# A routed-expert transformer layer: rows spread over the DMA queues, one sum in memory instead of two, and another order of the blocks

## What is computed

```python
h = modulate(rms_norm(x, ffn_norm_g), sh2, sc2)          # 512 x 1024
scores = sigmoid(h @ w_router)                            # 512 x 64
idx = top-8 experts of each token (4 of 8 groups of experts allowed)
w   = scores[idx] / sum * 2.5
routed[t] = sum over the 8 chosen e: w[t, e] * (silu(h[t] @ wg[e]) * (h[t] @ wu[e])) @ wd[e]
shared    = (silu(h @ wgs) * (h @ wus)) @ wds
out = x + g2 * (routed + shared)
```

## Time and profile before

| | us |
|---|---|
| median of 3 executions | 1282.87 |
| lowest and highest of them | 1282.39, 1285.67 |
| the profiled execution, its own time | 1285.91 |
| its span, first to last instruction | 1284.1 |

### The profile page before, as it was taken

One profiled execution on the slowest core, in us unless ns is written; L12 is line 12 of the kernel. 1 busy time (PEld: TensorE's weight loads), 2 busy tenths in 40 slices (PEclk: granted clock), 3 DMA queues, 4 the chain that ended last, 5 costly groups with the idle time before them and its releaser, 6 DMA issues.

```text
span 1284.1 us, 14047 instructions
## 1 busy us (share of the span) xinstructions
PE 1203.1 (94%) x4705; PEld 606.4 (47%) x4705; DVE 462.0 (36%) x1239; ACT 197.6 (15%) x452; POOL 193.3 (15%) x221
## 2 busy tenths in 40 slices
PE   6999999999999999998899998889999898999985
PEld 3444544444888544444444444333444343444442
DVE  2536557100666222555233323222323232233322
ACT  4110001011665001120001100000100010011100
POOL 0000000000221000100022323222222112223212
PEclk9999999999999999998899999988999899999998
DMA  8966661112100302167789999999999999989952
GB/s 275 368 217 229 219 231 65 66 65 83 50 0 1 131 1 106 72 256 290 278 294 364 383 386 378 382 364 375 370 300 379 386 363 391 384 291 381 358 135 35
DMA packets 88910, 311.52 MB, mean 243 GB/s; under 512 B 12400, under 2 KB 38160, under 8 KB 64912
## 3 DMA queue, kind: packets, MB, share of 16 engines
q1 hardware_dynamic: 72480, 272.77, 55.0%
q0 software_dynamic: 14784, 35.68, 11.8%
q10 hardware_dynamic: 1584, 2.27, 0.5%
HBM read 295.47 MB, written 34.08 MB: 257 GB/s over the span
## 4 chain that ended last, share of the span: by engine, by line
PE 80%; DMA 14%; DVE 2%; issue 1%; SPq 1%; ACT 1%; POOL 0%; DVEq 0%; POOLq 0%; ACTq 0%
PE PS L1718 21%; PE PS L1429 19%; PE PS L1739 11%; DMA R_HSA<-w_up_e 5%; DMA R_Z<-w_up_e 5%; PE PS L1597 4%; PE PS L1568 4%; PE PS L1704 3%; PE PS L1501 3%; PE PS L1477 2%; PE PS L1412 2%; DMA out<-second_sum 2%; DMA R_G<-h_rows,gidx 2%; PE PS L1607 2%; PE PS L1489 1%
## 5 line engine op out<-in xcount | busy, mean ns | idle before, releaser
L1429 PE MATMUL PS<-R_WT,R_HSA 128*128 128x512 f32 x576 | 248.2, 592 | 0.0
L1429 PEld LDWEIGHTS PS<-R_WT,R_HSA 128*128 128x128 f32 x576 | 109.3, 190 | 135.9 <-issue 135.8
L1265 DVE TENSOR_TENSOR R_G<-R_G,PS 128x256 f32<-128x256 f32 x50 | 30.4, 608 | 356.6 <-ACT R_G L864 356.6
L1718 PE MATMUL PS<-R_Z,R_G 128*64 128x512 f32 (+1 forms) x384 | 137.5, 603 | 13.0 <-DMA R_XM<-w_up_e 9.7
L1718 PE MATMUL PS<-R_WT,R_G 128*64 128x512 f32 (+1 forms) x352 | 129.1, 636 | 18.9 <-DMA R_WT<-w_up_e 10.9
L657 POOL DMA_INDIRECT R_G<-h_rows,gidx x54 | 56.3, 1042 | 431.6 <-DVE gidx L1254 370.5
L869 ACT ACTIVATE R_G<-PS 128x256 f32<-128x256 f32 x50 | 19.2, 383 | 556.2 <-PE PS L1726 556.2
L1286 DVE SCALAR_TENSOR_TENSOR R_G<-PS,slx,R_XM 128x512 f32<-128x512 f32 x100 | 74.9, 750 | 64.5 <-PE PS L1739 64.5
L1718 PEld LDWEIGHTS PS<-R_Z,R_G 128*64 128x64 f32 (+1 forms) x384 | 52.6, 161 | 92.9 <-issue 92.9
L1718 PE MATMUL PS<-R_XM,R_G 128*128 128x512 f32 (+1 forms) x192 | 88.0, 613 | 0.0
L1718 PEld LDWEIGHTS PS<-R_WT,R_G 128*64 128x64 f32 (+1 forms) x352 | 46.2, 163 | 84.7 <-issue 84.7
(11 more groups left out here) (256 smaller groups left out, 1318.6 us busy)
## 6 DMA issues: line engine op xcount, KB each, us to landing
R_Z<-w_gate_e SPq DMA_DIRECT2D x22, 1024.0 KB, 17.2
R_Z<-w_up_e SPq DMA_DIRECT2D x22, 1024.0 KB, 27.7
R_Z<-w_down_e SPq DMA_DIRECT2D x22, 1024.0 KB, 24.9
R_WT<-w_gate_e SPq DMA_DIRECT2D x21, 1024.0 KB, 16.6
R_WT<-w_up_e SPq DMA_DIRECT2D x21, 1024.0 KB, 30.1
R_WT<-w_down_e SPq DMA_DIRECT2D x21, 1024.0 KB, 27.1
R_WT<-ada_w SPq DMA_DIRECT2D x18, 1024.0 KB, 7.5
R_WT<-w_in SPq DMA_DIRECT2D x9, 2048.0 KB, 10.3
```

Source lines behind the costliest of these rows:

```text
L1265: dve.tensor_tensor(AR[:, b, :].rearrange("p (k d) -> p d k", k=2), by_line(SIL[:, b, :], 2), by_line(PS[:, b, F:2 * F], 2), ALU.mult).the ...
L1429: ins = mm(PS[:, t, :], HT[:, k, P * t:P * t + P], WR[:, b, k, :], start=k == 0, stop=k == KD - 1)
L1718: ins = mm(PS[w * h:w * h + w, b, :].rearrange("p (g n) -> p g n", g=2), XT[:, b, k, w * h:w * h + w], WGU[n][:, k], start=k == 0, stop=k ...
```

## The change

It does seven things.

- **Slots.** A new constant `slots` (loaded to `SLOTS` by one DMA of 224 KB on SyncE's queue, ahead of w_router) gives a block's rows other slot numbers: with 128 rows, rows 0, 8, 16, ... take slots 1 to 16, rows 1, 9, 17, ... take 17 to 32, and so on, so that the filled rows lie evenly over 16 groups of neighbouring rows. In every second single (`turned`) the groups count from the other end. A pair does this in each half with groups of four rows, the second half turned. For a narrow block, `onehot` now writes 96 slots and not 128.
- **One sum.** `second_sum`, `sum_order`, `sums_before` and `join_sums` are gone. All scatters add to `out`, and each waits until the one before has landed (`added`). A pair's second half waits for its first half on GpSimd.
- **Shared expert.** Its result is added to `out` by five accumulating DMAs from GpSimd (`add_shared`), between gather(1) and gather(2), in place of ScalarE's plain writes.
- **Start of GpSimd's loop.** gather(2) and gather(3) follow the shared adds; the waits for them to land stay before the first scatter.
- **Order of blocks.** `ORDER` spells out the 50 blocks; the pairs reach to the last one. `TAIL` is gone. The start is (0,), (1,), (30, 31), (7,), (8,), (32, 33), and the end is (58, 59), (27,), (60, 61), (28,), (29,), (62, 63). Three pairs in a row stand in two places.
- **Waits of VectorE.** `take_o` waits for the one count.
- **No drain.** The block is made with `no_gpsimd_drain=True`.

```diff
-TAIL = 6
+ORDER = "PWWPWWSWPWPPPWWPWWPSWWWPWWWPWWPPPWWPSPWPWWP"
 def block_order():
-    wide = [(j,) for j in range(7, NFULL - TAIL)]
-    half = [(j, j + 1) for j in range(NFULL, E, 2)]
-    apart = {3: [(2,), (64,)], 9: [(3,), (4,), (65, 66)], 15: [(5,), (6,), (67, 68)]}
+    wide = iter((j,) for j in range(7, NFULL))
+    half = iter((j, j + 1) for j in range(NFULL, E, 2))
+    apart = iter([[(2,), (64,)], [(3,), (4,), (65, 66)], [(5,), (6,), (67, 68)]])
     order = [(0,), (1,)]
-    for n, cols in enumerate(wide):
-        order += apart.get(n, []) + [cols] + half[n:n + 1]
-    return order + [(j,) for j in range(NFULL - TAIL, NFULL)]
+    for kind in ORDER:
+        order += next(apart) if kind == "S" else [next(wide if kind == "W" else half)]
+    return order
...
+ADDED = [sum(len(cols) for cols in COLS[:n]) for n in range(NM + 1)]
...
+def spread_slots(rows, turned):
+    row = np.arange(rows)
+    engine = row // (rows // 16)
+    return row % (rows // 16) * 16 + (15 - engine if turned else engine) + 1
...
-        block = st.enter_context(nc.Block())
+        block = st.enter_context(nc.Block(no_gpsimd_drain=True))
...
+        def turned(j, b):
+            return (j - PAIRS[j]) % 2 if isinstance(j, int) and j < NM else b
...
+        def added(j):
+            if isinstance(j, int) and j <= NM:
+                return 16 * ADDED[j]
+            return 16 * (j + (ADDED[NM] - NM))
...
+            sp.dma_start(SLOTS, a["slots"]).then_inc(s_ws, 16)
...
             def scatter(i, b):
                 j = 2 * i + b
                 pool.wait_ge(s_oe, 2 * j + 2)
                 pool.wait_ge(s_ri, copies(j + 1))
-                into = INTO[j] if isinstance(j, int) and j < NM else (0,)
-                for n in into:
-                    need(pool, s_sum[n], sums(n, j) + (16 if isinstance(j, int) and j == NM - TAIL else 0))
+                need(pool, s_sum, added(j))
                 settle(pool)
-                if len(into) == 1:
-                    add_rows(into[0], ridx[b], OB[0:rows(j), b, :])
+                if len(columns(j)) == 1:
+                    add_rows(ridx[b], OB[0:rows(j), b, :])
                 else:
-                    add_rows(0, ridx[b], OB[0:P // 2, b, :])
-                    add_rows(1, rhigh[b], OB[P // 2:P, b, :])
-            def join_sums():
-                pool.wait_ge(s_sum[1], sums(1, NM))
-                pool.wait_ge(s_sum[0], sums(0, NM - TAIL))
-                pool.dma_start(a["out"], sum_dram, accum_op=ALU.add, max_dma_last_dim=4 * D).then_inc(s_sum[0], 16)
-            for j in range(4):
-                gather(j, j % 2)
+                    add_rows(ridx[b], OB[0:P // 2, b, :])
+                    pool.wait_ge(s_sum, added(j) + 16)
+                    add_rows(rhigh[b], OB[P // 2:P, b, :])
+            def add_shared(t, ready):
+                pool.wait_ge(s_sx, ready)
+                for piece, at in SHARED_PIECES[t]:
+                    pool.dma_start(a["out"][P * t:P * (t + 1), at:at + piece.shape[1]], piece, accum_op=ALU.add)\
+                        .then_inc(s_sout[t % 2], 16)
+            gather(0, 0)
+            gather(1, 1)
+            pool.wait_ge(s_out, 16 * NT)
+            add_shared(1, 2)
+            add_shared(0, 4)
+            add_shared(2, 6)
+            add_shared(3, 8)
+            gather(2, 0)
+            gather(3, 1)
...
                 gather(j + 4, j % 2)
-                if j == NM - TAIL:
-                    join_sums()
                 scatter(j // 2, j % 2)
...
-            write_shared(1, 2)
-            write_shared(0, 4)
-            write_shared(2, 6)
             take_xt(0, 0)
             take_xt(1, 1)
-            write_shared(3, 8)
...
             def take_o(i, j, b):
-                if isinstance(j, int) and 2 <= j < NM:
-                    for n in INTO[j - 2]:
-                        dve.wait_ge(s_sum[n], sums(n, j - 1))
-                elif not isinstance(j, int) or j >= 2:
-                    dve.wait_ge(s_sum[0], sums(0, j - 1))
+                if not isinstance(j, int) or j >= 2:
+                    dve.wait_ge(s_sum, added(j - 1))
```

More of the change, by code:

```diff
@@ L123 @@
 C_N = C_SEL + HA
+S_WIDE = (0, P)
+S_NARROW = (2 * P, 2 * P + NARROW)
+S_N = 2 * P + 2 * NARROW
+def spread_slots(rows, turned):
+    row = np.arange(rows)
+    engine = row // (rows // 16)
+    return row % (rows // 16) * 16 + (15 - engine if turned else engine) + 1
 def constants():
@@ L134, in constants @@
     c[:, C_ONE:C_ONE + P] = 1.0
-    c[:, C_SLOT:C_SLOT + P] = f + 1
+    slots = np.zeros((P, S_N), np.float32)
+    for turned in range(2):
+        c[:, C_SLOT + P // 2 * turned:C_SLOT + P // 2 * turned + P // 2] = spread_slots(P // 2, turned)
+        slots[:, S_WIDE[turned]:S_WIDE[turned] + P] = spread_slots(P, turned)
+        slots[:, S_NARROW[turned]:S_NARROW[turned] + NARROW] = spread_slots(NARROW, turned)
     token = p + P * np.arange(NT)[None]
@@ L157, in constants @@
     causal[:, S - P:] = np.where(f > p, NEG, 0.0)
-    return c, causal
+    return c, causal, slots
 def build(nc, a):
@@ L337, in build @@
         s_gat = [sem(f"gathered{b}") for b in range(2)]
-        s_sum = [sem(f"added_to_sum{n}") for n in range(2)]
+        s_sum = sem("rows_added")
         s_ah, s_ohd, s_sl, s_xt, s_xtd, s_xta, s_gu, s_silu, s_act, s_at, s_ate, s_dn, s_oe, s_ri = map(sem, (
@@ L345, in build @@
         s_out = sem("residual_written")
-        s_sout = [sem(f"shared_written{b}") for b in range(2)]
+        s_sout = [sem(f"shared_added_to_out{b}") for b in range(2)]
         s_etab = sem("main_experts_ready")
@@ L660, in gather, with add_rows @@
                     bounds_check=S - 1, oob_is_err=False).then_inc(s_gat[b], 16)
-            def add_rows(n, index, part):
+            def add_rows(index, part):
                 pool.indirect_dma_start(
-                    out=sum_dram if n else a["out"],
+                    out=a["out"],
                     out_offset=bass.IndirectOffsetOnAxis(ap=index[0:part.shape[0], 0:1], axis=0),
                     in_=part, in_offset=None, compute_op=ALU.add,
-                    bounds_check=S - 1, oob_is_err=False).then_inc(s_sum[n], 16)
+                    bounds_check=S - 1, oob_is_err=False).then_inc(s_sum, 16)
             def scatter(i, b):
@@ L1801 @@
         give(name, array if name == "c" else array.reshape(array.shape[1:]))
-    for name, array in zip(("consts", "causal"), constants()):
+    for name, array in zip(("consts", "causal", "slots"), constants()):
         give(name, array)
```

24 lines of the change are left out of this document (10 added, 14 removed).

## The result

The changed kernel takes **1272.97 us** in the median (1268.80 to 1281.28, 11 runs) beside 1284.83 of the kernel before (11 runs): a ratio of 0.9915, 95% interval 0.9894 to 0.9935. It is faster by 0.9%, a quarter of what was forecast (1234 us). The time lies outside the range of 1220 to 1266. The profiled execution took 1276.11 us with a span of 1274.0; that of before had a span of 1284.1.

The account below looks back on a forecast made before the run. TensorE and the DMA engines were taken to bound the stage in turn, TensorE alone after the change: 1198.4 + 3 + 4 + 17.6 + 12.0 = 1235 us of span, so 1234 us, range 1220 to 1266.

Parts of the forecast that it names:

- Spread slots: Rows on DMA engines: spreading cuts q0's cost per byte from 1.96 to 1.40 of q1's, weights' work to 564 us.
- the work of 611 us: DMA engines from 600 us on: 259.9 MB, with q0's bytes priced at 1.96, at 425 GB/s.
- The third bound, the scatters: Chain of 69 scatters one at a time: 572 us against TensorE's 590, so hidden, with 3% to spare.
- a second half alone, 6: A pair's second scatter, issued alone: lands in 6 us, between 5.4 and 7.5.
- A single, 8.2: A single block's scatter: lands in 8.2 us with spread rows, 9.7 before, plus 0.95 to the next start.
- The second rival: Scatter chain paces, since spreading shortens no landing: chain 619 us, time 1265 us, kernel still gains; chance 0.13.
- its stated sign: VectorE's waits before ridx for a landing of out, over 10 us in all, would show rival 2 or 3.
- The first rival: Spread gives nothing and DMA engines pace: last weights at 1222 us, time 1250 us; chance 0.22.
- Rival 3: Scatter chain at the old landings of 8.8 us: 673 us, time 1318 us; chance 0.07 slower, 0.03 gain cancelled.
- The need for weights is level to the end: New block order without join: same bytes, TensorE's floor puts gate_up of block 49 at 1198.4 us.
- Shared rows: Five accumulating DMAs on GpSimd before gather(2): nothing if weights leave room, 8 us if not, 3 taken.
- The end: From gate_up of block 49: 17.6 us to VectorE's last product, then 12.0, the 6.28 us drain gone.

Follow-up runs that it names:

- e4: The kernel before with the slots table and the spread one-hots, nothing else; 1281.01 us, ratio to before 0.9957.
- e2: The changed kernel with the two sums and the join of before put back; order, spread and missing drain stay; 1272.36 us, ratio to before 0.9893.
- e12: The kernel with two sums, new order, spread slots and no drain, its join left out, so the second sum never reaches the output; 1264.74 us, one execution.
- e8: The kernel before with the new block order alone; two sums, join, drain and rows in place kept; 1288.76 us, ratio to before 1.0023.
- e7: The kernel before without GpSimd's drain at the end, nothing else changed; 1279.38 us, ratio to before 0.9958.
- e6: The changed kernel with scatters as plain writes, their addition left out; 1230.53 us, one execution.
- e13: The kernel with two sums, join, new order, spread slots and no drain, its scatters as plain writes, the join's addition kept; 1240.30 us, one execution.
- e9: Against the changed kernel: two sums, an order with eight singles last, the join in four pieces ahead of the 8th, 6th, 4th and 2nd block from the end; 1276.03 us.

## Why the prediction was wrong, point by point

**The failed step: "Spread slots".** It stands in two bounds, the DMA engines' work and a single's landing in the chain of scatters. The working took the measured price of a q0 byte (1.96 of q1's) and put it down to rows that crowd on few DMA engines, so that a spread would divide it by 1.4. A price was measured, its cause was assumed. The spread left it unchanged (22.1% before and after in e4). The addition in memory was most of the cause: by the queues' shares the price is 1.59 with it and 1.10 without, and the kernel then takes 1230.5 us. That is nearly the forecast's time, by another way: it was the time of a kernel whose DMA engines have room. The 1.96 itself is high, since the shares of the earlier trace rows give 1.61, but the work of 611 us is low: by the shares of the earlier trace rows, (69.3 + 22.2)% of 684.1 us, it is 626.

The prediction never priced the addition as something that could be the cause. The Trainium skill, "DMA: Bandwidth & Descriptors", section "SDMA does more than copy", says that each DMA engine has small compute units inline with the stream, an add among them; it gives no price, and the runs give one. The rule of the Trainium skill, "DMA: Bandwidth & Descriptors", section "The descriptor swizzle", by which each engine writes fixed partitions of a 128-partition transfer, was weighed against the spread. It came out on the right side (landings of 8.5 and 8.4 us with and without the spread), but no row shows which engine a row goes to, so the runs don't confirm it as the reason.

**Where the 38.5 us lie.** Block 49 was forecast at 1198.4 + 3 + 4 = 1205.4 and started at 1243.9. It is made of: block 2 at 642.5, where 644.3 + 3 was taken, -4.8; TensorE's own pace in the new order, 547.3 / 46 = 11.90 us a step in place of 11.79, +5 (both orders have nearly the same blocks, and over its first 12 steps, none of them late, before took 11.83, so up to 2 of these 5 may belong to the eight steps behind 11.79); lateness of 41.0 and 1.3 in the last step, where 4 were allowed, +38.3.

**The third bound, the scatters.** This is the bound that paced the changed kernel. The term "a second half alone, 6" measured 7.7 (median of 14 in 660 to 1180 us, 7.2 to 8.1), just above the upper bound of 7.5. "A single, 8.2" measured 10.0 (median of 24), as in before (10.3): it too rested on the spread. Over all 69 scatters the second halves took 7.2 us in the mean, which makes 23 of the 57 us between 572 and 629; the others took 8.6 where 7.9 had been put in, 37 us; shorter gaps gave 4 back. The second rival's working gave 619, and its stated sign came true: VectorE's waits ahead of ridx in 640 to 1280 us are 166 us, far over 10. It lacked those 23 us, and its other landings were 10 us too long in all. The prediction had also said that it is wrong if mean landings stay above 7.5: the mean of all 69 was 8.2. The first rival (the spread gives nothing, weights pace, 1250 us) was right on its cause too, and e2 and e12 show its limit with 28 to 30 us of lateness. Its time was early by the 15 us that the sum of the work lacked: the last weights landed at 1232.1 us in e12 and not at 1222. Neither rival was weighed together with the other, and each alone gave too early a time. Both true together had no case and no chance in the sum; the range ended at the one rival's own time. Rival 3 (1318 us, mean landing 8.8) had the landings among weights right (mean 8.7 in 660 to 1180 us) and its time too high: towards the end, with no weights moving, they fell to 3.5 to 5.2 us, and the mean of all, 8.2, is just under the 8.3 at which it would have cancelled the gain.

**Order.** "The need for weights is level to the end" was right and was paid: 12 us of lateness go with it in e8, 19 in e2 with the spread beside it. But the stalls at the two places with three pairs in a row, 4 us with a bound of 15 in the sum, are 28 us in e2, all of its lateness. The order gave little because the join, or in its place the chain, takes it back.

**Shared rows.** The 3 us never came: gather(2) was issued at 626.7 and landed at 635.1, before 641, and block 2 started 1.7 us earlier than in before. The five accumulating DMAs cost nothing that can be seen.

**The end.** Forecast 17.6 + 12.0 = 29.6 us, measured 30.1. The drain's 6.28 were 6.7 here and 6.7 in e7. This was the surest term and the one that carried the change. That the rest came out is luck, two errors that cancel. The wait for the scatter before, said to be gone, was there:

```profile
1261.24 0.75 DVE L1283 SCALAR_TENSOR_TENSOR R_G<-PS,slx,R_XM 128x512 f32<-128x512 f32 x1 [0.96 <-PE PS L1737]
...
1265.59 1.44 POOL L665 DMA_INDIRECT out<-R_G,ridx  x1 [2.70 <-DMA out<-R_G,ridx]
1269.88 1.42 POOL L665 DMA_INDIRECT out<-R_G,rhigh  x1 [2.85 <-DMA out<-R_G,ridx]
```

So the first half started 3.4 us later than forecast. The two landings of 3.5 us, in place of 4.8 each, gave 2.6 of it back.

**What came together.** The profiled spans differ by 10.1 us: the start -1.7, TensorE's own pace in the new order +5.0, lateness -6.3 (-19.3 by order and spread as e2 has it, +13.0 by the chain on one sum), the last step without the join -4.7, and the end -2.4 (the drain -6.7, and +4.3 that are left over, for a last pair's second half and its wait). The parts come from single executions and are good to a few us each.

## What to carry to other kernels

A price read from a trace is not its cause: before a change is forecast from it, name every way in which those bytes differ from the cheap ones (queue, pattern, addition), and ask which of them the change touches. When two limits lie within a few per cent of each other, give "both hold" a case of its own, with a later time than either alone. And price a gain that must pass an exclusive step, a join or a chain on one destination, only together with that step.

## What the runs showed of the hardware

A scatter that adds in memory takes far more of the DMA engines than a plain one. With it the scatter and gather queue costs 1.59 times the weights' queue per byte in 700 to 1100 us, without it 1.10, and the engines together move 387 GB/s in place of 361 (e6 against after) or 368 (e13 against e2). The gathers are in both figures, so the scatters' own ratio must be larger if the gathers' price is the same in both. The landing alone hides this: its median falls only from 9.3 to 8.4 us (e2 against e13).

A 2 MB join of two sums in memory, beside weights, took 27 us with the addition on its queue (26.9 us of waiting in e2) and moved its bytes in a stretch in which the DMA engines were full (share 1.03 in 1193 to 1219 us). Cut into four pieces in e9, the first two, beside weights, took 12.2 and 9.6 us, and the last two, with no weights moving, 5.1 and 5.6.
